# A decoder trunk on one core: a third pair of output blocks in block products, and value products moved in the softmax passes

## What is computed

```
y = rmsnorm(x) ; proj = y @ w_in
branches: stick-breaking (a), top-k sparse (b), NSA (c), dilated (d) attention
mix = sum over branches of sigmoid(gate_b) * (branch_b @ w_b)
h = x + mix @ w_out                    # the output projection
q = rmsnorm(h) @ wq ; top-k expert keys ; a = gelu(h @ U) ; out = h + (w * a) @ V
```

## Time and profile before

| | us |
|---|---|
| median of three runs | 1894.08 |
| the profiled execution, whole | 1893.71 |
| its span in the trace | 1891.9 |
| TensorE busy | 1887.2 (8855 matmuls) |
| VectorE busy | 1477.8 |
| ScalarE busy | 979.1 |

### The profile page before, as it was taken

One profiled execution on the slowest core, in us unless ns is written; L12 is line 12 of the kernel. 1 busy time (PEld: TensorE's weight loads), 2 busy tenths in 40 slices (PEclk: granted clock), 3 DMA queues, 4 the chain that ended last, 5 costly groups with the idle time before them and its releaser, 6 DMA issues.

```text
span 1891.9 us, 25741 instructions
## 1 busy us (share of the span) xinstructions
PE 1887.2 (100%) x8855; PEld 1560.3 (82%) x8855; DVE 1477.8 (78%) x2159; ACT 979.1 (52%) x1195; POOL 72.1 (4%) x109
## 2 busy tenths in 40 slices
PE   9999999999999999999999999999999999999999
PEld 8888878888888888888888888888888888888887
DVE  7578875685567889989765555899989978999897
ACT  7654644445466556546454464444444455555553
POOL 0010020210100000000000000000000000000000
PEclk9999999999999999999999999999999999999999
DMA  9976667767675569867887776767766678666664
GB/s 325 349 226 167 184 196 239 202 179 237 204 235 173 183 196 298 270 227 235 260 262 225 218 224 220 232 206 222 220 202 200 200 210 291 222 215 220 213 221 156
DMA packets 202384, 423.96 MB, mean 224 GB/s; under 512 B 46752, under 2 KB 125216, under 8 KB 201504
## 3 DMA queue, kind: packets, MB, share of 16 engines
q1 hardware_dynamic: 174048, 369.35, 62.9%
q0 software_dynamic: 7248, 27.92, 4.3%
q10 hardware_dynamic: 20976, 25.19, 3.9%
HBM read 395.79 MB, written 26.61 MB: 223 GB/s over the span
## 4 chain that ended last, share of the span: by engine, by line
PE 100%; DMA 0%; ACT 0%; DVE 0%; SPq 0%; issue 0%
PE acc L707 26%; PE acc L710 25%; PE acc L714 25%; PE acc L755 3%; PE acc L757 3%; PE acc L761 3%; PE acc L1193 2%; PE side L1072 1%; PE side L1071 1%; PE side L1073 1%; PE acc L1199 1%; PE acc L1113 1%; PE acc L1112 1%; PE acc L1118 1%; PE side L882 1%; PE side L999 1%
## 5 line engine op out<-in xcount | busy, mean ns | idle before, releaser
L1660 DVE TENSOR_TENSOR w_lo<-w_raw,w_hi 128x1024 fp32r<-128x1024 f32 (+1 forms) x649 | 784.9, 1213 | 367.6 <-ACT w_hi L1240 361.0
L1240 ACT ACTIVATE w_hi<-w_raw 128x1024 fp32r<-128x1024 f32 (+1 forms) x649 | 680.7, 1052 | 722.7 <-PE acc L714 585.7
L707 PE MATMUL acc<-w_hi,xt_hi 128*128 128x512 f32 x1348 | 366.4, 394 | 0.0
L710 PE MATMUL acc<-w_hi,xt_lo 128*128 128x512 f32 x1348 | 360.6, 389 | 0.0
L714 PE MATMUL acc<-w_lo,xt_hi 128*128 128x512 f32 x1348 | 360.5, 389 | 0.0
L710 PEld LDWEIGHTS acc<-w_hi,xt_lo 128*128 128x128 f32 x1348 | 253.1, 188 | 53.0
L707 PEld LDWEIGHTS acc<-w_hi,xt_hi 128*128 128x128 f32 x1348 | 251.3, 188 | 55.2 <-issue 4.9
L714 PEld LDWEIGHTS acc<-w_lo,xt_hi 128*128 128x128 f32 x1348 | 253.1, 188 | 52.8
L707 PE MATMUL acc<-w_hi,x_hi 128*128 128x512 f32 x640 | 173.5, 393 | 0.0
L710 PE MATMUL acc<-w_hi,x_lo 128*128 128x512 f32 x640 | 171.3, 390 | 0.0
L714 PE MATMUL acc<-w_lo,x_hi 128*128 128x512 f32 x640 | 171.2, 390 | 0.0
(11 more groups left out here) (387 smaller groups left out, 2076.0 us busy)
## 6 DMA issues: line engine op xcount, KB each, us to landing
w_raw<-in_stream SPq DMA_DIRECT2D x504, 512.0 KB, 4.2
w_raw<-in_w_in SPq DMA_DIRECT2D x16, 496.0 KB, 3.9
w_raw<-in_w_in SPq DMA_DIRECT2D x16, 480.0 KB, 5.2
w_raw<-in_w_in SPq DMA_DIRECT2D x16, 464.0 KB, 4.0
w_raw<-in_w_in SPq DMA_DIRECT2D x16, 448.0 KB, 4.2
w_raw<-in_w_in SPq DMA_DIRECT2D x16, 432.0 KB, 3.9
w_raw<-in_w_in SPq DMA_DIRECT2D x16, 416.0 KB, 4.6
w_raw<-in_w_in SPq DMA_DIRECT2D x16, 400.0 KB, 3.7
```

The lines of the kernel that those rows point to most:

```text
L707: pe.matmul(o[h], lhs(k0 + j, h)[0], wh[j], start=first and j == 0, stop=False)
L710: pe.matmul(o[h], lhs(k0 + j, h)[1], wh[j], start=False, stop=False)
L1240: nc.scalar.activation(w_hi[:, slot, 0:width], w_raw[:, slot, 0:width], ACT.Copy).then_inc(hi_ready, 1)
L1660: nc.vector.tensor_tensor(w_lo[:, slot, 0:width], w_raw[:, slot, 0:width], w_hi[:, slot, 0:width].bitcast(F32), ALU.subtract).then_inc(lo_ ...
```

## The change

It makes blocks 4 and 5 of the output projection a third pair, so that slots 64 to 95 are pair 2 and slots 96 to 127 two plain blocks. The pairs now have 3, 7 and 7 fast k pairs (2 and 6 before). The second group of activation sums takes in three k pairs instead of two. The differences' remainders (`out_t_lo`) move to a place that overlaps that of row block 1, so the rounding of row blocks 1 and later waits until all 17 fast products are done. Row blocks 1 to 5 are turned later. The x blocks of pair 2 are loaded after the 17th fast product, since their place is that of the differences. `add_pure` of pair 2 has its own place in slots 94 and 95. The value stage's pairs keep their products; only their numbers shift.

In the softmax passes the value product comes 12 chunks behind the scores for all passes (10 or 7 before), and three passes begin one or two chunks earlier.

```diff
-OUT_PAIRS = (Pair(0, CH_OUT, FAST[4:], 0), Pair(1, CH_OUT + 2 * CPG, FAST, 2))
-V_PAIRS = (Pair(2, CH_V, FAST_LAST[5:], 8), Pair(3, CH_F, FAST_LAST, 10), Pair(4, CH_F + 2 * CPG, FAST_LAST, 17),
-           Pair(5, CH_F + 4 * CPG, FAST_LAST, 24))
-OUT_PLAIN = CH_OUT + 4 * CPG
+OUT_PAIRS = (Pair(0, CH_OUT, FAST_LAST[4:], 0), Pair(1, CH_OUT + 2 * CPG, FAST_LAST, 3),
+             Pair(2, CH_OUT + 4 * CPG, FAST_LAST, 10))
+OUT_T = 17
+OUT_PLAIN = CH_OUT + 6 * CPG
...
-PASS_AT = (75, 82, 115, 121, 127, 133, 139, 145, 159, 165)
+PASS_AT = (75, 81, 115, 121, 127, 133, 139, 145, 157, 163)
...
-    out_s_hi = [at(f"out_s_hi{g}", [P, 4, 4 - 2 * g, P], F32R, PJ0 + (32 - 16 * g) * KB) for g in range(2)]
+    out_s_hi = [at(f"out_s_hi{g}", [P, 4, 4 - g, P], F32R, PJ0 + (30 - 18 * g) * KB) for g in range(2)]
...
-    out_t_lo = at("out_t_lo", [P, 2, 2, 512], F32R, PJ0 + 8 * KB)
+    out_t_lo = at("out_t_lo", [P, 2, 2, 512], F32R, PJ0 + 4 * KB)
...
-    ROW_END = {n: CH_OUT + {0: 2 * CPG, 1: 2 * CPG + 20, 2: 4 * CPG, 3: 4 * CPG + 10}.get(n, (n + 1) * CPG)
+    ROW_END = {n: CH_OUT + {0: 2 * CPG, 1: 4 * CPG + 14, 2: 4 * CPG + 22, 3: 6 * CPG - 4, 4: 6 * CPG + 4, 5: 6 * CPG + 10}.get(n, (n + 1) * CPG)
                for n in range(GRP)}
...
-                    if s == at_slot + (10 if i in BY_BLOCK else 7):
+                    if s == at_slot + 12:
                         weigh_values(i)
...
                 act.wait_ge(row_moved, 16 * (n + 1))
+                if n >= 1:
+                    act.wait_ge(t_used, OUT_T)
...
-                    if s == at_slot + (13 if i in BY_BLOCK else 10) and last_part(PASSES[i][0], PASSES[i][2]):
+                    if s == at_slot + 15 and last_part(PASSES[i][0], PASSES[i][2]):
                         out_hi(i)
...
-                k0, nq = 16 * g, 4 - 2 * g
+                k0, nq = 16 * g, 4 - g
...
-                if pair.fast[-1] == 12:
-                    for step, at in enumerate(((14, 1), (14, 1), (15, 0), (15, 1))):
+                late = pair.fast[-1] == 12
+                if late:
+                    when = ((15, 0), (15, 0), (15, 1), (15, 1)) if pair.order == 2 else ((14, 1), (14, 1), (15, 0), (15, 1))
+                    for step, at in enumerate(when):
...
                 if n == 4:
-                    pool.wait_ge(pure_free, 2)
+                    pool.wait_ge(t_used, OUT_T)
+                if n == 6:
+                    pool.wait_ge(pure_free, 3)
```

More of the change, by code:

```diff
@@ L516, in group_number @@
     def group_number(pair, i):
-        return GN_OUT + 2 * pair.order + i if pair in OUT_PAIRS else GN_V + 2 * (pair.order - 2) + i
+        return GN_OUT + 2 * pair.order + i if pair in OUT_PAIRS else GN_V + 2 * (pair.order - 3) + i
     def pair_bank(pair, i):
@@ L1078, in wait_block @@
             def wait_block(pair, i, h):
-                if pair.order > 2:
-                    pe.wait_ge(block_free, 4 * (pair.order - 3) + 2 * i + h + 1)
+                if pair.order > 3:
+                    pe.wait_ge(block_free, 4 * (pair.order - 4) + 2 * i + h + 1)
                 elif h == 0:
@@ L1123, in fast_products @@
                     pe.wait_ge(xt_lo_done, KT + kp + 1)
-                if pair.order == 2:
+                if pair.order == 3:
                     pe.wait_ge(wmat_lo, kp + 1)
-                if first and pair.order in (1, 3, 4, 5):
+                if first and pair.order in (1, 2, 4, 5, 6):
                     pe.wait_ge(pure_free, pair.order)
-                if first and pair.order == 2:
+                if first and pair.order == 3:
                     pe.wait_ge(gates_put, ROUNDS)
                 if first:
-                    pe.wait_ge(s_lo_done, 12 if pair.order >= 2 else 8)
+                    pe.wait_ge(s_lo_done, 12 if pair.order >= 3 else 8)
                 def to_c21():
@@ L2248, in between @@
                             block_probs(i)
[L2249 removed]
+                    if s == at_slot + 16 and last_part(PASSES[i][0], PASSES[i][2]):
                         out_lo(i)
@@ L2354, in t_sums @@
                     dve.wait_ge(t_lo_done, 2 * n)
-                if kp == pair.fast[0] and pair.order == 2:
+                if kp == pair.fast[0] and pair.order == 3:
                     dve.wait_ge(s_lo_done, 12)
-                if kp == pair.fast[0] and pair.order in (1, 3, 4, 5):
+                if kp == pair.fast[0] and pair.order in (1, 2, 4, 5, 6):
                     dve.wait_ge(pure_free, pair.order)
@@ L2388, in block_rows_of @@
                     return rows[:, h, n * 512:(n + 1) * 512]
-                n = 2 * (pair.order - 2) + i
+                n = 2 * (pair.order - 3) + i
                 return h_rows[:, h, n * 512:(n + 1) * 512]
             def add_pure(pair, step):
-                u, v = (t[:] for t in (out_sums if pair in OUT_PAIRS else sums))
+                u, v = (t[:] for t in (out_sums[pair.order] if pair in OUT_PAIRS else sums))
                 p1, p5, p6, p7 = (side[:, i, :] for i in range(4))
@@ L2449, in pair_tasks @@
                         t_sums(after, 0)
-                if kp in (13, 14) and pair.fast[-1] < 12:
+                if kp in (13, 14) and not late:
                     add_pure(pair, 2 * (kp - 13) + i)
@@ L2477, in _ @@
                 if pair:
-                    pair_tasks(pair, kp, i, {0: OUT_PAIRS[1], 2: V_PAIRS[1]}.get(pair.order))
+                    pair_tasks(pair, kp, i, {0: OUT_PAIRS[1], 1: OUT_PAIRS[2], 3: V_PAIRS[1]}.get(pair.order))
                 between(s)
             for pair in V_PAIRS[1:]:
-                before = V_PAIRS[pair.order - 3]
-                after = V_PAIRS[pair.order - 1] if pair.order < 5 else None
+                before = V_PAIRS[pair.order - 4]
+                after = V_PAIRS[pair.order - 2] if pair.order < 6 else None
                 for kp in range(CPG):
```

18 lines of the change are left out of this document (10 added, 8 removed).

## The result

| | before | after |
|---|---|---|
| median of nine runs each | 1894.08 us (1893.52 to 1895.06) | 1898.05 us (1896.71 to 1899.83) |
| the profiled execution | 1893.71 us | 1896.71 us |
| its span | 1891.9 us | 1894.9 us |

The ratio is 1.0021, 95% interval 1.0013 to 1.0029: 4.0 us slower, just past the 0.2% at which I had drawn the line. I had forecast 1893.6 us, no change. The time lies in the range; the direction is wrong.

What follows compares the result with a forecast made beforehand. TensorE was taken to bound the kernel from end to end. From 1893.71 us, - 6.12 + 5.6 + 0 gave 1893.2, and 0.37 for the median made 1893.6 us; the 8-in-10 range was 1888.0 to 1898.6.

Steps and rivals of the forecast that it cites:

- Part 1: Output projection: nine more fast k pairs, each three matmuls less, 27 x 0.2267 = 6.12 us less on TensorE; called certain.
- Part 2: Side work of the output projection's fast k pairs: VectorE's idle time before slot 13 covers larger sums; 0, at most 1 us.
- Part 3: End of the third pair, slots 90 to 98: work queued behind ScalarE's held rounding makes TensorE wait 5.6 us before slot 96.
- Part 4: Softmax passes: value products 12 slots behind their scores add no wait; taken as 0, with a gain of at most 1.7 us.
- (B): Rival, third pair's end: held ScalarE costs little, stall 0.8 us, 1888.8 us in all, or 1888.0 without stall; chance 0.26.
- (C): Rival, third pair: x blocks 4 and 5 land late for `add_pure`, 1898.6 us, or 1896.6 by the port rule; chance 0.14.

Runs made afterwards that it cites:

- the kernel with the bank first: Output projection's part alone with rows turned later, plus bank-freeing additions at slot 95 and `add_pure` steps 3 and 4 at slots 96 and 97: 1889.62 us, ratio 0.9977.
- the first experiment: The changed kernel with the softmax passes placed as before, so the output projection's part alone: 1897.43 us, ratio 1.0014.
- the kernel with later row blocks: Output projection's part alone, with row block 1's rounding moved to slots 98 and 99 and turning of blocks 2 to 6 behind slot 98: 1894.88 us, ratio 1.0004.
- The fill: Output projection's part alone, plus 18 unused matmuls into a free bank while TensorE waits for plain block 6's bank: 1895.30 us, ratio 1.0003.
- the kernel with the 2.15 us: Output projection's part alone with rows turned later, plus the two bank-freeing additions moved from slot 98 to slot 96: 1892.01 us, ratio 0.9989.

## Why the prediction was right or wrong, point by point

**Part 1, right.** The page counts 8828 matmuls, 27 fewer than before. Pair 2 runs from 927.69 to 1010.17 (when slot 96 was due), 82.5 us, 4.6 less than 32 plain slots; 4.76 was said, and 0.15 of the difference are two small gaps.

**Part 2, within or somewhat over its bound.** I took 0 and at most 1 us. It was 0.7 us in the changed kernel's trace, 1.1 in the kernel with the bank first, and 2.0 in the first experiment's. The largest gaps are where the prediction said to look, and one has a releaser named in the waits (`out_t_lo` on VectorE, 0.26 us at 805.26 with the bank first). The step that failed is that VectorE's idle time before slot 13 would cover it: 1.46 us of idle time still stand there (it was 1.03 us at that place), while products behind it come late. That idle time was no reserve. ScalarE stands in its queue until the sums are made (6.66 us at 792.27), its weight roundings come behind that, and VectorE idles because they are late. Larger sums move all of this back, by 1.6 us counted from slot 0 (794.83 - 759.81 against 792.10 - 758.69), and VectorE then has no idle time up to the two `out_t_lo` of slots 16 and 17. It begins the first at 804.31 and needs 1.2 us for it, and TensorE wants it at 805.37.

**Part 3, right to 0.1 us as a wait, and short by what follows it.** Counted from 993.84, the start of slot 90:

| | forecast | measured |
|---|---|---|
| ScalarE's rounding of rows begins | 0.26 | 0.26 |
| remainder of slot 91 begins | 2.2 | 2.2 |
| remainder of slot 92 begins | 5.6 | 5.5 |
| `add_pure` begins | 10.05 | 9.9 |
| bank free | 21.9 | 21.8 |
| TensorE's wait | 5.6 | 5.5 |

Its two steps 1 and 2 of `add_pure` are 2.69 us by its own terms (1.28 + 1.41), not the 2.75 that it put in; 2.76 were measured, so this slip did no harm. Each wait that I had named is in the rows: ScalarE released by L1076, VectorE idle for 5.86 us before it, one wait of TensorE on the additions. What the sum has not is a term for the clock. I priced the idle time, and TensorE also runs at 1.2 GHz in the first work behind it: 1.7 us in the changed kernel, 1.5 in the first experiment, some 2.9 in the kernel with later row blocks. The fill shows that the two can be parted: the bank as late, no half clock, 2.1 us less between the medians. This missing term is the largest part of the error.

**Part 4, wrong.** I took 0, with a gain of up to 1.7 us as the only bound, and wrote that a later scores product can't cost since it has the roundings of three slots in front of it. The scores of the sixth pass need more than roundings: they wait for the copy of the fifth pass's probabilities, and that copy was moved as well, from chunk 135 to 137, behind a value product moved to 133 and behind ScalarE's own rounding. I had looked at what each moved step waits for, and not at the chain through all three. It costs 0.9 us in the trace and 1.0 us alone on the chip, and goes with a shift by one chunk.

**The rivals.** (B), that the held ScalarE costs little, didn't come: the wait is 5.5 us, and the rows tie it to the hold step by step. Taking the hold away gave 3.8 us of idle time rather than (B)'s 0.8, because (C)'s transfers came next. (C) didn't set the time of the changed kernel, for there VectorE begins `add_pure` only at 1003.77, 9.2 us after POOL's issue at 994.57. The landing of the loads in that stretch of the changed kernel, from least to most:

```profile
DMA to landing us min/median/max: 4.1/4.5/5.9
```

But its price was nearer than I thought. I bounded one load at 7.4 us and called both hidden by 8.4, while in the later kernels the pair needs 7.6 to 9.0 us, with `add_pure` due at about 10. In those kernels VectorE was standing idle for 4 to 5 us while the loads were under way, so it wasn't an engine that blocked them, and the rule of the Trainium skill that I had weighed there (page "SBUF — State Buffer", section "SBUF: two separate sides") doesn't explain their lateness. The trace shows SyncE's weight loads beside them (1.15 MB against 0.22 MB of x in 4 us), and none in the changed kernel. That my bound held there was luck in part: I hadn't seen that the held ScalarE also holds back the weight loads. That all eight x loads before landed in stretches with VectorE busy for nearly nine tenths was misread too: rows 9 cover three of the eight, and in the 6 us from each of the last four VectorE is busy for 46 to 79%.

**The sum again.** -6.1 + 5.6 was right in both terms. Missing were +1.7 (clock), +0.9 (pass) and +0.7 (small gaps): 1893.2 + 3.3 = 1896.5 us, against 1896.71 us of the profiled execution. So three steps failed: the stall priced as idle time alone, the moved passes put at 0, and VectorE's idle time taken as cover. Between the medians another 1.0 us is missing, since the median of the changed kernel lies 1.3 us above its profiled execution and I had added 0.37.

**Open.** Why the median of the changed kernel is 1.3 us above its profiled execution, where before it is 0.4. The small gaps (0.7 to 2.2 us in the kernels with this wait) and the length of the half clock (3 to 6 us) both differ between traces, and either would do; the untraced runs can't say which, for their mean clock, 0.998 in eight of nine, is the same at 1896.71 and at 1899.83 us.

## What to carry to other kernels

When a saturated TensorE gets one long wait, price the wait and the half clock behind it, and bring the wait down to where the clock stays up before counting any saved products as won. Read a stall as a queue: the engine in order that is held first, all that stands behind its waiting instruction, and the one release that the bottleneck needs. That release can be taken out of the queue's end; here that, together with the rows turned later and the passes left as they were, turned 4.0 us of loss into 4.5 us of gain. Idle time of an engine is a reserve only if nothing upstream of it is held by the work that you add. And an engine that is late also holds back the transfers that refill what it frees, so making it early can make another transfer late. When steps of a pipeline are moved by the same number of slots, check the chain through all of them, not each one's own wait, for two of them may land in one slot with a third engine between.

## What the runs showed of the hardware that I had not expected

- One idle time of 5.3 or 5.5 us in a kernel that otherwise keeps TensorE busy throughout was followed by work at 1.2 GHz that cost 1.7 and 1.5 us; one of 3.8 us cost 2.9 us in that way. Idle times of 1.15 and 2.15 us left it at 2.4 GHz in their traces; in two of the eleven runs of the kernel with the 2.15 us the mean clock is 0.999, so it can fall there too.
- Eighteen useless matmuls in the wait kept the clock up (mean 1.000 in eleven of eleven runs) and made the kernel 2.1 us faster than without them.
- Two loads of 512 KB issued together on POOL's queue landed after 7.6 and 8.0 us, and 8.1 and 9.0 us, with VectorE idle for most of that time, where the same loads had landed in 4.1 to 7.4 us before the change and in 4.1 to 5.9 us in the changed kernel. In their first 4 us, SyncE's weight loads moved 1.15 MB beside the late pair of the kernel with the bank first, nothing beside the pair of the changed kernel, and 0.50 to 0.88 MB beside the single loads of before. That isn't all of it: a single x load took 8.1 us in the kernel with the sixth pass moved, with 0.61 MB beside it.
